# At each layer boundary, the sums of squares of x are taken as columns of tokens with the squares as weights, instead of as rows streamed through ones

## The chip, the cores and the metric

The kernel runs on one core of one Trainium2 chip. The metric is the device time of one launch in microseconds; the median of three runs is used. All arithmetic is fp32 (products are written as three fp32r products of high and low parts).

## The reference, cut to what matters

Two layers of a diffusion backbone over 512 latent tokens and 256 context tokens of width 1024 (layer 0 mixes with grouped-query attention, layer 1 with a Hyena long convolution; each is followed by a squared-ReLU MLP). Around every mixer and every MLP stands the same piece, and the change is in it:

```python
def rmsnorm(x, g):
    y = xf * lax.rsqrt(jnp.mean(xf * xf, axis=-1, keepdims=True) + RMS_EPS)
    return y * g
def sandwich_update(x, y_mix, mod, g, w1, w2):
    x = x + mod[2] * rmsnorm(y_mix, g[1])
    h = modulate(rmsnorm(x, g[2]), mod[3], mod[4])
    return x + mod[5] * rmsnorm(sq_relu_mlp(h, w1, w2), g[3])
```

So at the end of each mixer or MLP, y is normalised by its own root mean square and added to x, and x is normalised again for what comes next. The sum of squares of x over the 1024 channels, one number for each of the 512 tokens, is what the change computes in another way.

## The kernel before, in words

Activations are held transposed: x, y and the operands hhi and hlo are tiles of 128 channels by 8 chunks by 512 tokens. A weight matrix is cut into units: a unit is 8 chunks of 128 x 128 weights and gives 128 output channels for 512 tokens, with three products for each chunk (high by high, high by low, low by high; L1760, L1761, L1762 in the helper that the profile names). Each weight unit is loaded by SP, cut into high and low parts by ScalarE (L695) and VectorE (L1127), and multiplied by TensorE. The program of every engine is written out by hand, with semaphores between them; the order within an engine is the order of its code. There are four boundaries b = 0 to 3 (after attention, after MLP 0, after Hyena, after MLP 1). The last, b = 3, only adds y to x; the sums of squares of x are taken at the first three.

A boundary runs as follows (function `boundary` of each engine, and `first_units` of TensorE).

- **y's root.** TensorE's `square_column` (L1984) sums y's squares with a narrow product: the squares (128 x 128) are the weights, and one column of ones is streamed (L1989), after a product of 64 rows that writes zeros (L1987). An fp32 product is recorded as two matmuls, so a call with 4 columns of 128 tokens gives 8 records. ScalarE takes the root (L939), VectorE its reciprocal (L1451), and TensorE spreads it over 128 rows (`root_rows`, L1997). Around this, `keep_busy` (L2001, records at L2004) issues products of 512 columns whose result nobody reads: 3 before, 3 between, 10 after.
- **x.** VectorE scales y (`y_scale`, L1465) and adds it to x (`x_add`, L1470) in four parts: two halves of 256 tokens (`HALVES`), each in two groups of four chunks. ScalarE squares x into y's place (L951), two chunks at a time. TensorE sums the squares over the channels in `x_sums` (L2023, records at L2029): the weights are a 128 x 128 tile of ones, the squares of one chunk and half (128 x 256) are streamed, and 8 chunks accumulate in `XSUM[h]`, so that each of 128 rows holds all 256 sums.
- **x's root.** VectorE's `x_column` (L1472) turns the rows into columns of tokens: for each 128 tokens it multiplies the 128 x 128 block of the sums with the identity and adds along the row (L1477, then a read-out of the accumulator), which leaves the diagonal in `xcol`. ScalarE takes the root of two columns (`x_root`, L961), VectorE the reciprocal (`x_inverse`, L1484), TensorE spreads it to rows (`x_rows`, L2033, records at L2036).
- **Operands.** VectorE multiplies x by gain and root (`half_scaled`, L1488), ScalarE adds the shift and rounds to hhi (L969), VectorE gets hlo (`half_lo`, L1493).
- **First units.** TensorE then runs the first three units of the next matrix chunk by chunk for half 0 and then half 1 (`first_units`), with `x_rows` of half 1 after chunk 3 of half 0.

The order of VectorE within a boundary is: four parts of scale and add, with `x_column(0)` ahead of the last scale and `x_inverse(0)` ahead of the last add; then the products of half 0, with `x_column(1)` at chunk 3 and `x_inverse(1)` at chunk 5; then half 1. The order of TensorE is `x_sums(b, 0)`, the first four chunks of `x_sums(b, 1)`, `x_rows(b, 0)`, the last four chunks, the first units.

Of the kernel before, what the change touches and what calls it, by code (L numbers as in the profile page):

```python
# [27 lines left out]
ALU = mybir.AluOpType  # L28
ACT = mybir.ActivationFunctionType
AX = mybir.AxisListType  # L30

P = 128
D = 1024
KC = D // P
NT = 512
NC = 256
# [6 lines left out]
QT = NT // P  # L43
EPS = 1e-6
FH = 64
# [43 lines left out]
def build(nc, xT, ctxT, cT, cols, wpack, ahead, apack, fw1, fw2, fw3, featsT, skips, decay, tables, consts, ropes, fdram, out):  # L89
    with ExitStack() as ctx:  # L90
        def sb(name, shape, dt=F32, stack=ctx):
            return stack.enter_context(nc.sbuf_tensor(name, shape, dt))

        def sem(name):
            return ctx.enter_context(nc.semaphore(name))
# [17 lines left out]
        S = sb("scratch", [P, 12, NT])  # L113
# [12 lines left out]
        rq = sb("rq", [P, NH * QT])  # L126
        bmax = sb("bmax", [P, 2])
        nroot = sb("nroot", [P, QT])
        xcol = sb("xcol", [P, QT])
        xroot = sb("xroot", [P, QT])  # L130
        epst = sb("eps", [P, 1])
        tap2 = sb("tap2", [P, 2, NT])
        ident, ones = (cst[:, n, :] for n in range(2))
        y = S[:, 0:KC, :]
# [23 lines left out]
        with ExitStack() as area:  # L158
            t2hi = sb("t2hi", [P, 6, NT], F32R, area)
# [10 lines left out]
        B2 = ctx.enter_context(nc.psum_tensor("bank2", [P, NT], F32))  # L170
        B3 = ctx.enter_context(nc.psum_tensor("bank3", [P, NT], F32))
        SC = ctx.enter_context(nc.psum_tensor("bank45", [P, 2, NT], F32))
        SD = ctx.enter_context(nc.psum_tensor("bank67", [P, 2, NT], F32))
# [22 lines left out]
        inverse_done = sem("inverse_done")  # L196
        row_done = sem("row_done")
        xsum_done = sem("xsum_done")
        xcol_done = sem("xcol_done")
        xroot_done = sem("xroot_done")  # L200
        xinverse_done = sem("xinverse_done")
        xrow_done = sem("xrow_done")
# [120 lines left out]
        for u in range(QKV_UNITS):  # L323
            if u in UNIT_Q:
                h = UNIT_Q.index(u)
# [72 lines left out]
        FIRST_BANKS = (AB[:, 0, :], AB[:, 1, :], SC[:, 0, :], B2[:, :])  # L398
        X_GROUPS = 4
        HALVES = (slice(0, NC), slice(NC, NT))  # L400
        XSUM = (B2[:, 0:NC], SD[:, 0, 0:NC])
        XROWS = (SD[:, 1, 0:NC], SC[:, 1, 0:NC])

        def operand_base(b):
# [4 lines left out]
        def f(ap):  # L409
            return ap.bitcast(F32)  # L410
# [275 lines left out]
        def _(act):  # L686
            own = Own(act, own_act)
            A = nc.scalar.activation
# [147 lines left out]
            for t in range(QKV_UNITS + 2):  # L836
# [7 lines left out]
                for n, (_, ps, w, r, key, hi, lo) in jobs_of(t - 1):  # L844
# [3 lines left out]
                    else:  # L848
                        h, w = UNIT_Q.index(t - 1), QT
# [9 lines left out]
                for i, (n, (_, ps, w, r, key, hi, lo)) in enumerate(jobs_of(t)):  # L859
# [6 lines left out]
                    if key:  # L866
                        ins = A(value_of(n), ps, ACT.Copy)
                    else:
                        h = UNIT_Q.index(t)
                        if h >= 3:  # L870
                            act.wait_ge(job_full, jobs_of(UNIT_Q[h - 3])[0][1][3] + 1)
                        ins = A(value_of(n), ps, ACT.Copy, scale=qg[:, 0:1])
# [84 lines left out]

            def x_root(b, h):

                act.wait_ge(xcol_done, 4 * b + 2 * h + 2)  # L960
                A(xroot[:, 2 * h:2 * h + 2], xcol[:, 2 * h:2 * h + 2], ACT.Sqrt, scale=1.0 / D,  # L961
                  bias=epst[:, 0:1]).then_inc(xroot_done, 1)

            def half_his(b, h, js):
# [153 lines left out]
        def _(dve):  # L1118
# [299 lines left out]
            for n in range(NQ + 6):  # L1418
# [10 lines left out]
                if 0 <= m < NQ:  # L1429
                    dve.wait_ge(phi_done, m + 1)  # L1430
                    at = slice((m % 2) * P, (m % 2 + 1) * P)
# [16 lines left out]
            def inverse(m):  # L1448

                dve.wait_ge(root_done, m + 1)  # L1450
                nc.vector.reciprocal(nroot[:, :], nroot[:, :]).then_inc(inverse_done, 1)  # L1451

            def boundary(b):
                lo_, no_, ls, ts = BOUND[b][2:]
                inverse(b)
                if b % 2:
                    dve.wait_ge(yg_done, KC * (b // 2 + 1))
                else:
                    dve.wait_ge(evac_done, (U_OUT0, U_OUT1)[b // 2] + KC)
                dve.wait_ge(row_done, b + 1)  # L1460

                def y_scale(h, g):
                    at, js = HALVES[h], slice(4 * g, 4 * g + 4)
                    rows = B3[:, at].unsqueeze(1).broadcast_to([P, 4, NC])
                    TT(y[:, js, at], y[:, js, at], rows, ALU.mult).then_inc(scaled_done, 1)  # L1465

                def x_add(h, g):
                    at, js = HALVES[h], slice(4 * g, 4 * g + 4)
                    dve.wait_ge(scaled_done, X_GROUPS * b + 2 * h + g + 1)
                    TT(x[:, js, at], x[:, js, at], y[:, js, at], ALU.add).then_inc(x_done, 1)  # L1470

                def x_column(h):  # L1472
                    dve.wait_ge(xsum_done, 2 * b + h + 1)
                    for c in range(2):
                        if b or h or c:
                            dve.wait_ge(xcol_done, 4 * b + 2 * h + c)
                        nc.vector.tensor_tensor_reduce(S[:, 8, 0:P], XSUM[h][:, c * P:(c + 1) * P], ident, 1.0, 0.0,  # L1477
                                                       ALU.mult, ALU.add,
                                                       xcol[:, 2 * h + c:2 * h + c + 1]).then_inc(xcol_done, 1)

                def x_inverse(h):
                    dve.wait_ge(xroot_done, 2 * b + h + 1)
                    half = xroot[:, 2 * h:2 * h + 2]
                    nc.vector.reciprocal(half, half).then_inc(xinverse_done, 1)  # L1484

                def half_scaled(h, j):
                    at = HALVES[h]
                    STT(y[:, j, at], x[:, j, at], gcol(lo_, no_, j), XROWS[h], ALU.mult, ALU.mult).then_inc(ht_done, 1)  # L1488

                def half_lo(h, j):  # L1490
                    at = HALVES[h]
                    dve.wait_ge(hhi_done, operand_base(b) + KC * h + j + 1)
                    STT(hlo[:, j, at], y[:, j, at], shift(ls, ts, j), f(hhi[:, j, at]), ALU.add,  # L1493
                        ALU.subtract).then_inc(h_done, 1)

                if b == 3:
                    for i in range(X_GROUPS):
                        js = slice(2 * i, 2 * i + 2)
                        rows = B3[:, :].unsqueeze(1).broadcast_to([P, 2, NT])
                        TT(y[:, js, :], y[:, js, :], rows, ALU.mult).then_inc(scaled_done, 1)  # L1500
                        dve.wait_ge(scaled_done, X_GROUPS * b + i + 1)
                        TT(x[:, js, :], x[:, js, :], y[:, js, :], ALU.add).then_inc(x_done, 1)  # L1502
                    return
                y_scale(0, 0)
                x_add(0, 0)
                y_scale(0, 1)
                x_add(0, 1)
                y_scale(1, 0)
                x_add(1, 0)
                x_column(0)  # L1510
                y_scale(1, 1)
                x_inverse(0)
                x_add(1, 1)
                for h in range(2):
                    dve.wait_ge(xrow_done, 2 * b + h + 1)
                    dve.wait_ge(x_done, X_GROUPS * b + 2 * h + 2)
                    for j in range(KC + 1):
                        if j < KC:
                            half_scaled(h, j)
                        if j:  # L1520
                            half_lo(h, j - 1)
                        if h == 0 and j == 3:
                            x_column(1)
                        if h == 0 and j == 5:
                            x_inverse(1)
                    if h == 0:
                        prep(NEXT_UNIT[b] + AHEAD, AHEAD, AHEAD % 2)
# [40 lines left out]
            for j in range(OUT_UNITS):  # L1568
# [3 lines left out]
                if j in (1, 3, 5):  # L1572
                    third = j // 2
                    at = slice(2 * third, 2 * third + 2)
# [180 lines left out]
        def _(pe):  # L1755
            mm = nc.tensor.matmul
# [146 lines left out]
            for t in range(QKV_UNITS + 2):  # L1903
# [18 lines left out]
                for n, (_, ps, w, r, key, hi, lo) in jobs_of(t - 1):  # L1922
# [8 lines left out]
                    for qt in range(QT):  # L1931
                        ins = mm(B2[:, qt:qt + 1], S[:, 4 + n % 2, qt * P:(qt + 1) * P], ones[:, 0:1],  # L1932
                                 start=True, stop=True)
# [18 lines left out]
            for n in range(NQ + 5):  # L1952
                m = n - 3
                if 0 <= m < NQ:
                    pe.wait_ge(p_done, m + 1)
                    pe.wait_ge(exp_done, min(n - 1, NQ))
                    for kt in range(KT):
                        ins = nc.tensor.transpose(turned(m)[:, kt * P:(kt + 1) * P],  # L1958
                                                  PROB[m % 2][:, kt * P:(kt + 1) * P], ident)
                    ins.then_inc(pt_done, 1)  # L1960
                if n < NQ:
                    h, qt = divmod(n, QT)
# [43 lines left out]
            def boundary(b):  # L2006
                if b == 0:
                    pe.wait_ge(thi_done, 4)
                keep_busy(3)
                pe.wait_ge(yacc_done, (KC - 2) * (b + 1))  # L2010
                if b:
                    pe.wait_ge(xcol_done, 4 * b)
                if b == 2:
                    pe.wait_ge(tap_done, HY_UNITS)
                square_column(S[:, 11, :], True, False)
                pe.wait_ge(ysq_done, KC * (b + 1))
                square_column(S[:, 10, :], False, True).then_inc(col_done, 1)
                keep_busy(3)
                root_rows(b)
                if b < 3:  # L2020
                    keep_busy(10)

            def x_sums(b, h, js=range(KC)):  # L2023
                at = HALVES[h]
                if h == 0:
                    pe.wait_ge(root_done, b + 1)
                for j in js:
                    pe.wait_ge(xsquare_done, KC * b + 4 * h + j // 2 + 1)
                    ins = mm(XSUM[h], ones, y[:, j, at], start=j == 0, stop=j == KC - 1)  # L2029
                if js[-1] == KC - 1:  # L2030
                    ins.then_inc(xsum_done, 1)

# [244 lines left out]
```

## Time and profile before

| | before |
|---|---|
| median of 3 runs | 1406.29 us (1404.71 to 1406.71) |
| the profiled execution, its own time | 1407.46 us |
| its span, first to last instruction | 1405.7 us |
| TensorE busy | 1366.5 us, 97% |
| VectorE, ScalarE, GpSimd busy | 63%, 43%, 9% |
| granted clock of TensorE, mean | 0.993 of full speed |
| share of the chain that ended last | TensorE 84%, VectorE 7% |

The span is 1.8 us shorter than the execution's time. The busy time of an engine is the union of its instructions; a record of a matmul includes its way through the array, so that successive matmuls overlap, and what one costs is the step from its start to the next one's. The granted clock is a share of 2.4 GHz: 1.00 is 2.4 GHz and 0.50 is 1.2 GHz.

### The profile page before, as it was taken

What the parts mean: (1) busy time and instruction counts of PE and PEld (TensorE: products, weight loads), DVE (VectorE), ACT (ScalarE), POOL (GpSimd) and SP (SyncE); (2) the same over time, 40 slices, a digit from 0 to 9 for tenths busy, and PEclk for the clock granted to TensorE, in tenths of its full rate; (3) what the DMA queues carried; (4) which work ended last, traced back from release to release, by engine and by line L of the source; (5) the groups of instructions that cost most, each with busy time, mean ns of one, the idle gap of its engine ahead of it and who ended that gap; (6) DMA issues with size and microseconds to landing.
All of it is one profiled execution on the core that took longest, in us unless ns stands there. A gap on an engine that the chain in (4) does not pass through costs nothing.

```text
span 1405.7 us, 18116 instructions
## 1 busy us (share of the span) xinstructions
PE 1366.5 (97%) x6676; PEld 1124.2 (80%) x6676; DVE 890.2 (63%) x1279; ACT 608.4 (43%) x903; POOL 123.1 (9%) x151
## 2 busy tenths in 40 slices
PE   9989998999999999999999999999999999999996
PEld 2568787988888888888879888888888888888885
DVE  6898779977865555555457999997274333333333
ACT  3655446664462432514435433433446143341541
POOL 1761120002000000000110000000200000000011
PEclk9999999999999999999999999999999999999998
DMA  9535251119266565565321222231303222223221
GB/s 361 218 141 175 82 167 52 46 46 320 84 210 209 180 209 180 193 199 176 104 90 61 75 105 76 90 120 36 119 27 120 94 95 97 94 99 104 90 75 60
DMA packets 48330, 178.47 MB, mean 127 GB/s; under 512 B 5928, under 2 KB 6248, under 8 KB 45834
## 3 DMA queue, kind: packets, MB, share of 16 engines
q1 hardware_dynamic: 45194, 164.51, 34.3%
q0 software_dynamic: 3072, 13.11, 2.9%
q8 instruction: 39, 0.64, 0.2%
q14 instruction: 25, 0.20, 0.0%
HBM read 164.49 MB, written 10.49 MB: 124 GB/s over the span
## 4 chain that ended last, share of the span: by engine, by line
PE 84%; DVE 7%; issue 1%; ACT 1%; POOL 0%; DVEq 0%; POOLq 0%; ACTq 0%
PE bank L1760 27%; PE bank L1762 26%; PE bank L1761 26%; PE bank L1958 2%; PE bank L2029 1%; DVE x L1470 1%; DVE scratch L1465 1%; PE bank L1989 1%; PE bank L2004 0%; PE bank L1932 0%; PE bank L2111 0%; PE bank L1997 0%; DVE x L1502 0%; DVE glo L1663 0%; DVE scratch L1500 0%
## 5 line engine op out<-in xcount | busy, mean ns | idle before, releaser
L1760 PE MATMUL bank<-hhi,whi 128*128 128x512 f32 (+1 forms) x1000 | 376.8, 377 | 0.4 <-DVE wlo L1127 0.4
L1762 PE MATMUL bank<-hhi,wlo 128*128 128x512 f32 (+1 forms) x1000 | 374.2, 374 | 0.0
L1761 PE MATMUL bank<-hlo,whi 128*128 128x512 f32 (+1 forms) x1000 | 373.9, 374 | 0.0
L695 ACT ACTIVATE whi<-raw 128x1024 fp32r<-128x1024 f32 x180 | 189.1, 1053 | 231.8 <-PE bank L1762 199.9
L1127 DVE TENSOR_TENSOR wlo<-raw,whi 128x1024 fp32r<-128x1024 f32 x180 | 222.4, 1237 | 91.8 <-ACT whi L695 90.3
L1760 PEld LDWEIGHTS bank<-hhi,whi 128*128 128x128 f32 x1000 | 188.4, 188 | 34.0 <-issue 1.2
L1762 PEld LDWEIGHTS bank<-hhi,wlo 128*128 128x128 f32 x1000 | 188.3, 188 | 34.0
L1761 PEld LDWEIGHTS bank<-hlo,whi 128*128 128x128 f32 x1000 | 188.4, 188 | 32.8
L1762 PE MATMUL bank<-ghi,wlo 128*128 128x512 f32 x512 | 199.2, 389 | 0.0
L1760 PE MATMUL bank<-ghi,whi 128*128 128x512 f32 x512 | 199.2, 389 | 0.0
L1761 PE MATMUL bank<-glo,whi 128*128 128x512 f32 x512 | 199.2, 389 | 0.0
L1544 DVE TENSOR_TENSOR glo<-scratch,ghi 128x512 fp32r<-128x512 f32 x64 | 44.3, 693 | 173.7 <-ACT ghi L990 173.7
L1762 PEld LDWEIGHTS bank<-ghi,wlo 128*128 128x128 f32 x512 | 96.1, 188 | 20.1
L1761 PEld LDWEIGHTS bank<-glo,whi 128*128 128x128 f32 x512 | 96.1, 188 | 20.0
L1760 PEld LDWEIGHTS bank<-ghi,whi 128*128 128x128 f32 x512 | 96.1, 188 | 19.8
L662 POOL TENSOR_TENSOR scratch<-scratch 128x512 f32<-128x512 f32 x24 | 33.1, 1381 | 831.9 <-ACT scratch L917 831.9
L986 ACT ACTIVATE scratch<-bank 128x512 f32<-128x512 f32 x64 | 38.1, 596 | 151.8 <-PE bank L1762 151.8
L1556 DVE TENSOR_TENSOR scratch<-scratch,bank 128x512 f32<-128x512 f32 x48 | 33.0, 687 | 109.2 <-PE bank L1762 109.2
L1415 DVE CUSTOM_DVE_ANT_0 araw<-araw,crow 128x1024 f32<-128x1024 f32 x36 | 43.5, 1218 | 0.0
L1415 DVE CUSTOM_DVE_ANT_0 amore<-amore,crow 128x1024 f32<-128x1024 f32 x36 | 43.5, 1216 | 0.0
L988 ACT ACTIVATE scratch<-scratch 128x512 f32<-128x512 f32 x64 | 40.5, 632 | 2.0
L990 ACT ACTIVATE ghi<-scratch 128x512 fp32r<-128x512 f32 x64 | 40.5, 632 | 2.0
(275 smaller groups left out, 1968.7 us busy)
## 6 DMA issues: line engine op xcount, KB each, us to landing
raw<-in_wpack SPq DMA_DIRECT2D x180, 512.0 KB, 3.5
araw<-in_apack SPq DMA_DIRECT2D x40, 512.0 KB, 3.5
amore<-in_apack SPq DMA_DIRECT2D x36, 512.0 KB, 3.5
ablk<-in_ahead SPq DMA_DIRECT2D x8, 1024.0 KB, 11.6
spectra<-scratch SPq DMA_DIRECT2D x16, 512.0 KB, 3.2
araw<-spectra POOLq DMA_DIRECT2D x8, 1024.0 KB, 5.1
fs<-in_fw SPq DMA_DIRECT2D x2, 1024.0 KB, 11.2
x<-in_xT SPq DMA_DIRECT2D x1, 2048.0 KB, 12.5
```

Source lines behind the costliest of these rows:

```text
L662: nc.gpsimd.tensor_tensor(S[:, 11, :], S[:, 11, :], S[:, 10, :], ALU.add).then_inc(yacc_done, 1)
L695: A(whi[:, s, :], raw[:, r, :], ACT.Copy).then_inc(hi_done, 1)
L986: A(S[:, 8 + j % 2, :], bank, ACT.Relu).then_inc(evac_done, 1)
L988: A(S[:, 10 + j % 2, :], S[:, 8 + j % 2, :], ACT.Square).then_inc(g_full, 1)
L990: A(ghi[:, j, :], S[:, 10 + j % 2, :], ACT.Copy).then_inc(ghi_done, 1)
L1127: TT(wlo[:, s, :], raw[:, r, :], f(whi[:, s, :]), ALU.subtract).then_inc(lo_done, 1)
L1415: nc.vector.tensor_tensor_reduce(slot, slot, crow if early else crow1[:, :], 1.0, 0.0, ALU.mult, ALU.add, dst).then_inc(arow_done, 1)
L1544: TT(glo[:, j, :], S[:, 10 + j % 2, :], f(ghi[:, j, :]), ALU.subtract).then_inc(g_done, 1)
L1556: TT(y[:, j, :], y[:, j, :], AB[:, j % 2, :], ALU.add).then_inc(evac_done, 1)
L1760: mm(o, lh, rh, start=first, stop=False)
L1761: mm(o, lh, rl, start=False, stop=False)
L1762: return mm(o, ll, rh, start=False, stop=last)
```

## The change

The row sums of x become column sums. In `x_sums`, the squares of one chunk and 128 tokens are the weights and one column of ones is streamed, into one column for each 128 tokens (`XCOLS[h]`, two columns of a bank). Ahead of each half a product of 64 rows writes zeros into the two columns. After every second chunk one product of 256 columns is issued whose result nobody reads. ScalarE's `x_root` reads the two columns where they are and waits for the sums; `x_column`, the tile `xcol` and the semaphore `xcol_done` are gone. At the start of a later boundary TensorE waits for the roots of the one before it instead of its columns.

```diff
-        XSUM = (B2[:, 0:NC], SD[:, 0, 0:NC])
+        XCOLS = (B2[:, 0:2], SD[:, 0, 0:2])
...
             def x_root(b, h):
 
-                act.wait_ge(xcol_done, 4 * b + 2 * h + 2)
-                A(xroot[:, 2 * h:2 * h + 2], xcol[:, 2 * h:2 * h + 2], ACT.Sqrt, scale=1.0 / D,
+                act.wait_ge(xsum_done, 2 * b + h + 1)
+                A(xroot[:, 2 * h:2 * h + 2], XCOLS[h], ACT.Sqrt, scale=1.0 / D,
                   bias=epst[:, 0:1]).then_inc(xroot_done, 1)
...
-                def x_column(h):
-                    dve.wait_ge(xsum_done, 2 * b + h + 1)
-                    for c in range(2):
-                        if b or h or c:
-                            dve.wait_ge(xcol_done, 4 * b + 2 * h + c)
-                        nc.vector.tensor_tensor_reduce(S[:, 8, 0:P], XSUM[h][:, c * P:(c + 1) * P], ident, 1.0, 0.0,
-                                                       ALU.mult, ALU.add,
-                                                       xcol[:, 2 * h + c:2 * h + c + 1]).then_inc(xcol_done, 1)
-
...
                 x_add(1, 0)
-                x_column(0)
                 y_scale(1, 1)
...
-                        if h == 0 and j == 3:
-                            x_column(1)
...
                 if b:
-                    pe.wait_ge(xcol_done, 4 * b)
+                    pe.wait_ge(xroot_done, 2 * b)
...
                 if h == 0:
                     pe.wait_ge(root_done, b + 1)
+                if js[0] == 0:
+                    mm(XCOLS[h], ones[0:FH, :], ident[0:FH, P - 2:P], start=True, stop=False)
                 for j in js:
                     pe.wait_ge(xsquare_done, KC * b + 4 * h + j // 2 + 1)
-                    ins = mm(XSUM[h], ones, y[:, j, at], start=j == 0, stop=j == KC - 1)
+                    for c in range(2):
+                        ins = mm(XCOLS[h][:, c:c + 1], y[:, j, at][:, c * P:(c + 1) * P], ones[:, 0:1], start=False,
+                                 stop=j == KC - 1 and c == 1)
+                    if j % 2:
+                        mm(SC[:, 0, 0:NC], t2hi[:, 0, 0:P], t2hi[:, 1, 0:NC], start=True, stop=True)
                 if js[-1] == KC - 1:
                     ins.then_inc(xsum_done, 1)
```

## Rows read from the trace of the kernel before

**Rows 1.** The page: busy time of each engine, and the chain by line.

```profile
PE 1366.5 (97%) x6676; PEld 1124.2 (80%) x6676; DVE 890.2 (63%) x1279; ACT 608.4 (43%) x903; POOL 123.1 (9%) x151
...
PE bank L1760 27%; PE bank L1762 26%; PE bank L1761 26%; PE bank L1958 2%; PE bank L2029 1%; DVE x L1470 1%; DVE scratch L1465 1%; PE bank L1989 1%; PE bank L2004 0%; PE bank L1932 0%; PE bank L2111 0%; PE bank L1997 0%; DVE x L1502 0%; DVE glo L1663 0%; DVE scratch L1500 0%
```

**Rows 2.** Busy time by stretch (start:end, length, engines), the first boundary and its first units.

```profile
361.00:371.46 10.46, 8.01 (x35) 6.35 (x36) 9.17 (x15) 5.58 (x11) 0.00 (x0) 1.00 0.00 1
371.49:389.30 17.81, 17.81 (x150) 17.78 (x149) 13.22 (x35) 8.71 (x17) 0.00 (x0) 1.00 0.10 31
```

**Rows 3.** The line of x's sums, all of its matmuls (ns min/median/max, starts).

```profile
L2029 PE MATMUL bank<-scratch,consts x96: 379/379/483, 361.8 to 1037.0; 128*128 128x256 f32 x96
```

**Rows 4.** Timeline of the first boundary (start us, us, engine, line; idle before, releaser).

```profile
358.14 2.56 PE L2004 MATMUL bank<-t2hi 128*128 128x512 f32 x10
...
364.08 1.99 PE L2029 MATMUL bank<-scratch,consts 128*128 128x256 f32 x8 [0.33 <-ACT scratch L951]
364.52 1.23 DVE L1470 TENSOR_TENSOR x<-x,scratch 128x1024 f32<-128x1024 f32 x1
...
366.11 0.29 DVE L1477 CUSTOM_DVE_ANT_0 scratch<-bank,consts 128x128 f32<-128x128 f32 x1 [0.36 <-PE bank L2029]
...
366.47 1.99 PE L2029 MATMUL bank<-scratch,consts 128*128 128x256 f32 x8 [0.40 <-ACT scratch L951]
...
366.84 0.28 ACT L961 ACTIVATE xroot<-xcol,eps 128x2 f32<-128x2 f32 x1
367.79 0.16 DVE L1484 RECIPROCAL xroot<-xroot 128x2 f32<-128x2 f32 x1
...
368.08 0.63 PEld L2036 LDWEIGHTS bank<-consts,xroot 128*128 128x128 f32 x4
...
369.05 0.87 DVE L1488 SCALAR_TENSOR_TENSOR scratch<-x,gain,bank 128x256 f32<-128x256 f32 x2
369.17 1.15 ACT L951 ACTIVATE scratch<-x 128x512 f32<-128x512 f32 x2 [2.04 <-DVE x L1470]
...
369.85 1.99 PE L2029 MATMUL bank<-scratch,consts 128*128 128x256 f32 x8 [0.94 <-ACT scratch L951]
...
370.75 0.48 DVE L1493 SCALAR_TENSOR_TENSOR hlo<-scratch,mods,hhi 128x256 fp32r<-128x256 f32 x1 [0.83 <-ACT hhi L969]
...
371.49 0.47 PE L1760 MATMUL bank<-hhi,whi 128*128 128x256 f32 x1
```

**Rows 5.** Timeline of y's column sums, at the first and the second boundary.

```profile
354.64 1.95 PE L1989 MATMUL bank<-consts,scratch 128*128 128x1 f32 x16
...
356.63 0.26 ACT L939 ACTIVATE nroot<-bank,eps 128x4 f32<-128x4 f32 x1 [1.72 <-PE bank L1989]
356.99 0.18 DVE L1451 RECIPROCAL nroot<-nroot 128x4 f32<-128x4 f32 x1 [2.40 <-ACT nroot L939]
...
722.05 0.38 PE L1987 MATMUL bank<-consts 64*128 64x4 f32 x2
...
724.17 1.39 PE L2004 MATMUL bank<-t2hi 128*128 128x512 f32 x3
```

**Rows 6.** Busy time by stretch; behind POOL's, the granted clock of TensorE.

```profile
352.39:359.22 6.83, 6.83 (x43) 5.70 (x42) 3.04 (x8) 1.44 (x3) 0.00 (x0) 1.00 0.81 301
721.03:724.45 3.42, 3.42 (x24) 2.94 (x23) 1.43 (x6) 1.46 (x3) 0.00 (x0) 1.00 0.95 370
724.45:727.86 3.41, 3.41 (x13) 3.03 (x12) 0.66 (x2) 0.16 (x1) 0.00 (x0) 0.50 0.16 64
...
1390.05:1393.45 3.40, 2.70 (x11) 2.21 (x9) 0.77 (x2) 0.10 (x1) 0.00 (x0) 0.50 0.00 0
```

**Rows 7.** Timeline, the eight broadcasts of y's root at the first and second boundary.

```profile
357.23 1.15 PE L1997 MATMUL bank<-consts,nroot 128*128 128x128 f32 x8
...
725.35 1.91 PE L1997 MATMUL bank<-consts,nroot 128*128 128x128 f32 x8
```

More of the change, by code:

```diff
@@ L128, in build @@
         nroot = sb("nroot", [P, QT])
-        xcol = sb("xcol", [P, QT])
         xroot = sb("xroot", [P, QT])
@@ L198, in build @@
         xsum_done = sem("xsum_done")
-        xcol_done = sem("xcol_done")
         xroot_done = sem("xroot_done")
```

## The prediction

> **What bounds the kernel.** I read the page first: TensorE is busy 97% of the span, and 79% of the chain that ended last is the three products of a unit, L1760 to L1762 [rows 1]. So a microsecond counts only if TensorE loses it. The page's line of the granted clock is not flat, so I read the clock by stretches later. Then I read the table of stretches around one boundary. In the 10.46 us from the first scaled x to the end of its sums TensorE has 8.01 us busy; in the 17.81 us of the first units behind it, it is busy throughout; the clock is full in both [rows 2]. VectorE and ScalarE are ahead once the first units run, so what the change saves them there is worth nothing. What matters is when the first unit starts, and at what clock TensorE gets there. The line of the sums has 96 records, 32 at each of three boundaries [rows 3], so each term below comes three times. The timeline of the first one follows; the others repeat it to 0.02 us.
>
> **The path in that boundary** [rows 4]. TensorE sums half 0 (eight records, 364.08 to 366.07). VectorE takes the diagonal twice, 366.11 on, then does the last scaling, the reciprocal (367.79) and the last add of x. ScalarE squares (369.17), TensorE sums the last four chunks (369.85), and the first unit's first matmul starts at 371.49. Its operand is ready sooner: hlo starts at 370.75 and takes 0.48, so 371.23. In this last step TensorE itself is the bound.
>
> **Removed and added, at full clock.** (1) Sums. A wide block of four chunks is 8 records; from its first to the next weights is 1.61 us (366.47 to 368.08, where the rows of roots load theirs) [rows 4]. A narrow record, a square as weights and one column streamed, is that of L1989: 16 in 1.95 us, the last 0.25, so (1.95 - 0.25)/15 = 0.113 us each [rows 5]. A new block is 16 of them and 2 fillers of 256 columns. No such filler is in the trace; bounds are 0.12, what a 256-column product of the first units takes (150 records in 17.81 us [rows 2]), and 0.26, what each of the ten 512-column fillers takes (2.56 us together) [rows 4]. I take 0.12, of the same width. 16 x 0.113 + 2 x 0.12 = 2.05 us, or 0.44 more than before, per block. The zeroing product of two columns costs about what L1987 does, 0.38 us [rows 5], and for both halves is issued while TensorE waits for squares: nothing. If that cover went, it would be 0.3 us.
> (2) Half 0's sums: 364.08 + 2.05 = 366.13 for the last narrow one's end, against 366.07. A narrow result reaches ScalarE 0.04 us after its end (L1989 ends 356.59, the root starts 356.63 [rows 5]), but ScalarE's own squares hold the root at 366.84 as before [rows 4]. Reading PSUM instead of a column costs it nothing: 0.26 us at L939 [rows 5] against 0.28.
> (3) Two diagonals leave VectorE, about 0.3 us each, and with them the 0.36 us of waiting before them [rows 4]. The scaling starts behind the add of 364.52, that is at 365.7. It ends before the root, for which the reciprocal now waits: 366.84 + 0.28 + 0.10 for the signal (what lies between 356.63 + 0.26 and the reciprocal at 356.99 [rows 5]) = 367.22, instead of 367.79. Late next is that root. The last add and its squares come 0.57 us earlier, the last block starts at 369.28 instead of 369.85 and ends at 369.28 + 2.05 = 371.33 against 371.47: a gain of 0.14.
> (4) The rows of roots wait behind the longer block on TensorE: 366.47 + 2.05 = 368.52 instead of 368.08. They reach VectorE at 369.3, not 369.05. Queued behind that wait are half 0's products and ScalarE's hhi; hhi stands behind ScalarE's squares anyway (368.60 + 1.15 = 369.75), so hlo is done at 370.8, still 0.5 us ahead of TensorE.
> (5) Half 1's diagonals (0.6 us of VectorE at 372.7) lie under the first units: nothing. No DMA changes, the SP and POOL queues are not touched, and the new wait before the next boundary's columns (roots done, not columns done) was met hundreds of microseconds before.
> Sum at full clock: 3 x -0.14 = -0.4 us; from 0 to -1.7 (if all of the 0.57 came through).
>
> **The clock.** Not one wide matmul is left between the ten fillers that end at 360.7 [rows 4] and the first unit, but eight of 256 columns and four broadcasts. The trace shows what narrow ones do. From 721.03 to 724.45 TensorE is busy 3.42 of 3.42 us, most of it (722.05 to 724.17 [rows 5]) narrow records between wide fillers, at the full 2.4 GHz; the next stretch, 724.45 to 727.86, is granted 0.50, that is 1.2 GHz. At the last boundary the same work is followed by 0.50 from 1390.05. At the first it leaves the clock at 1.00 [rows 6]. So 2 us of narrow records among wide ones cost the clock in some of the blocks. The new stretch is 10 us long, at all three boundaries. I forecast that it falls in each.
> The Trainium skill ("TensorE: Matmul & The Clock Gate", Why this matters for your kernels) ties a fall to idle gaps between bursts of matmuls; TensorE would have no gap much over 1 us in the new boundary, so by that rule the clock holds and the time is that of the second rival, 1405.9. The trace does not agree: TensorE was never without work from 721.03 to 724.45 and its clock fell [rows 6].
> Price: eight broadcasts take 1.15 us at 2.4 GHz, 1.91 at 1.2 [rows 7]: with the last one's 0.28 and 0.42 taken off, (1.91 - 0.42)/7 = 0.213 us a record instead of (1.15 - 0.28)/7 = 0.12, for the same loads of 128 weights that bound a narrow record, which goes from 0.113 to the same 0.213. So a block costs 18 x 0.10 = 1.8 us more, the rows of roots 0.4. The falls shown come 2.4 us after narrow work began (722.05 to 724.45); here it begins at 361.7, so a fall may come from 363 to 367, and I take 366. Block 1.8, rows 0.4, block 1.8, less 0.35 because no wait for squares is left between, less 0.14: the first unit starts 3.5 us later, at 375.0. One low stretch lasts 3.41 us [rows 6], so the third would begin at 372.8 and end at 376.2: 1.2 us of first units at half speed, 0.6 lost: 4.1 us. If that third one, mostly narrow, is followed by a fourth, 1.7 more: 5.8. I take the middle, 4.9. Ends: two low stretches only, 2 x 1.7 less 0.35 and what else was idle, 2.6; four, with the fall before 364 so that the root is late too, 7.2. Behind the boundary TensorE bounds, so nothing is won back.
> Sum: 3 x 4.9 = 14.7. The profiled execution took 1407.46 (span 1405.7 and 1.8 around it), 1.2 above the median; it would be 1422.2, and for the median 1406.3 + 14.7 = 1421.0. Ends 3 x 2.6 and 3 x 7.2: 1414 and 1428.
>
> **Rivals.** A measurement tells about 0.2%, 2.8 us, from no change.
> - **Falls only in part**: at one or two boundaries, or a single low stretch each (1.7 less the 0.5 that is idle now, three times 1.2). The block at 354 that kept its clock speaks for it; that the new stretch is four times as long against. 1409 to 1414, chance 0.20.
> - **The clock holds**: fillers or weight loads are enough. For it: two fillers in every block, and no moment without weights. Against: three 512-column fillers ahead of the narrow records of 722 and more behind them were not enough. 1406.3 - 0.4 = 1405.9, chance 0.14.
> - **Faster**: the clock holds, and the operands that VectorE makes, not TensorE's sums, set the pace from the start of the first unit on. Then all that VectorE is rid of counts: four diagonals of 0.3 us and the wait of 0.36, 1.6 us at each boundary, 4.8 in all: 1401.5. It decides from the point where the last block takes less than 1.5 us, since hlo is there at 370.8: (1.5 - 0.24)/16 = 0.08 for a narrow record, against the 0.113 of L1989. Chance 0.04.
>
> **The numbers.** Forecast (falls at all three, two to four low stretches each) 0.62, in part 0.20, holds 0.14, faster 0.04. Range 1409 to 1429: it takes in the first two and leaves out 0.18. Slower by over 0.2% is 0.62 + 0.20 = 0.82; within 0.2% 0.14; faster 0.04.
>
> **What would show it.** In the profile after: no rows of the diagonal; narrow records of the sums at 0.11 us, later at 0.21; the granted clock 0.50 for some 7 to 10 us from about 366, and likewise near 735 and 1032; the first unit starts at 375 instead of 371.5. In the half where the clock is full, the last add comes 0.5 us earlier. The forecast is wrong if the clock stays at 1.00 between the sums and the first unit; then the first unit should start at 371.3.

## The result, and the profile after

| | before | after |
|---|---|---|
| median | 1406.50 us (4 runs, 1404.71 to 1407.98) | 1424.62 us (4 runs, 1423.08 to 1428.05) |
| profiled execution, its own time | 1407.46 us | 1425.49 us |
| its span | 1405.7 us | 1423.4 us |
| granted clock, mean | 0.993 | 0.977 |

The changed kernel is slower: ratio 1.0136, 95% interval 1.0123 to 1.0149; by the medians 18.1 us. 1421.0 was forecast, 1409 to 1429 was the range.

The page after: busy time of each engine, the granted clock in 40 slices, and the chain by line (L1746 to L1748 are the three products that were L1760 to L1762; L2018 is the narrow record of x's sums, L2021 its filler).

```profile
PE 1390.2 (98%) x6808; PEld 1152.0 (81%) x6808; DVE 887.7 (62%) x1255; ACT 608.5 (43%) x903; POOL 123.2 (9%) x151
...
PEclk9999999999799999999998999999979999999998
...
PE bank L1746 26%; PE bank L1748 26%; PE bank L1747 26%; PE bank L2018 2%; PE bank L1944 2%; PE bank L2021 1%; PE bank L1975 1%; PE bank L1918 0%; DVE x L1468 0%; PE bank L1990 0%; DVE scratch L1463 0%; PE bank L2103 0%; DVE x L1491 0%; DVE glo L1649 0%; DVE scratch L1489 0%
```

VectorE has 2.5 us less to do than in [rows 1], and that changed nothing. TensorE is busy 23.7 us longer although it streams far fewer columns. The first three dents in the line of the clock lie in the slices of the three boundaries; the 8 in the last slice stands in the page of the kernel before too. The busy time by stretch, changed kernel, shows them in full (the number behind POOL's is the granted clock):

```profile
358.02:362.54 4.52, 3.84 (x24) 3.05 (x22) 4.10 (x4) 1.15 (x2) 0.00 (x0) 1.00 0.04 15
362.54:383.02 20.48, 20.48 (x96) 20.24 (x96) 13.33 (x24) 8.76 (x17) 0.00 (x0) 0.50 0.00 1
383.02:397.84 14.82, 14.82 (x126) 14.82 (x126) 6.56 (x16) 4.50 (x9) 0.00 (x0) 1.00 0.10 36
...
741.42:755.07 13.65, 13.65 (x64) 13.41 (x63) 8.84 (x20) 6.24 (x14) 0.00 (x0) 0.50 0.01 1
...
1034.97:1038.38 3.41, 3.41 (x14) 3.07 (x13) 1.17 (x1) 0.00 (x0) 0.00 (x0) 0.50 0.00 0
...
1045.21:1058.86 13.65, 13.65 (x65) 13.63 (x65) 9.22 (x21) 6.79 (x14) 0.00 (x0) 0.50 0.00 1
```

At each boundary TensorE runs at 1.2 GHz for 13.65 or 20.48 us, where [rows 2] has 1.00 throughout. It is without a pause in these stretches. The other three executions of the changed kernel have a mean granted clock of 0.975 to 0.978, like this one. The timeline of the first boundary, changed kernel, to be laid beside [rows 4]; its last two lines are where the narrow records of the second and third boundary begin:

```profile
361.56 1.05 PE L2018 MATMUL bank<-consts,scratch 128*128 128x1 f32 x8 [0.68 <-ACT scratch L949]
...
362.79 1.70 PE L2018 MATMUL bank<-consts,scratch 128*128 128x1 f32 x8
...
368.37 0.26 ACT L959 ACTIVATE xroot<-bank,eps 128x2 f32<-128x2 f32 x1 [1.55 <-PE bank L2018]
368.66 0.17 DVE L1473 RECIPROCAL xroot<-xroot 128x2 f32<-128x2 f32 x1 [1.90 <-ACT xroot L959]
...
373.20 1.06 PE L2028 MATMUL bank<-consts,xroot 128*128 128x128 f32 x4
...
374.30 0.87 DVE L1477 SCALAR_TENSOR_TENSOR scratch<-x,gain,bank 128x256 f32<-128x256 f32 x2 [4.35 <-PE bank L2028]
...
375.35 0.48 DVE L1482 SCALAR_TENSOR_TENSOR hlo<-scratch,mods,hhi 128x256 fp32r<-128x256 f32 x1 [0.18 <-ACT hhi L967]
...
377.89 0.41 PE L1746 MATMUL bank<-hhi,whi 128*128 128x256 f32 x1
378.11 0.41 PE L1747 MATMUL bank<-hlo,whi 128*128 128x256 f32 x1
378.32 0.41 PE L1748 MATMUL bank<-hhi,wlo 128*128 128x256 f32 x1
...
737.84 1.05 PE L2018 MATMUL bank<-consts,scratch 128*128 128x1 f32 x8 [0.71 <-ACT scratch L949]
...
1040.40 1.05 PE L2018 MATMUL bank<-consts,scratch 128*128 128x1 f32 x8
```

Eight narrow records take 1.05 us ahead of the fall and 1.70 behind it. The fall comes 0.98 us after the first narrow record at this boundary, 3.58 and 4.81 us after it at the other two. The root of half 0 comes at 368.37 instead of 366.84, now because its sums are late. VectorE waits 4.35 us for the rows of roots, and the first unit starts at 377.89 instead of 371.49. It does not wait for its operand (375.35 + 0.48), but for TensorE's own sums.

To compare executions I measure each boundary from the first of the ten fillers to the first unit, and on to the first product of 512 columns, with which the three first units are over. Each is the difference of two starts in the timeline:

| | to the first unit | to the end of the first units | low clock up to that end |
|---|---|---|---|
| before | 13.35, 13.46, 13.35 | 31.25, 31.35, 31.24 | 0, 0.94, 0 |
| after | 19.88, 18.25, 17.33 | 39.82, 37.07, 37.13 | 20.48, 13.65, 13.65 + 1.62 |

The three boundaries lost 8.57, 5.72 and 5.89 us, 20.2 in all. The span grew by 17.7, because elsewhere this execution was 2.5 us shorter. 1.5 of them lie at y's sums, ahead of the fillers of the three boundaries and in the last boundary: the kernel before had stretches at 0.50 at 724.45 and 1390.05 [rows 6], and this execution of the changed kernel had none where they stood, only one at 1034.97. Another 0.8 lie between the second and the third boundary, in the products from 820 to 968 of the kernel before, and 0.1 ahead of the first boundary; the change has no code in either place, and their cause is open.

### The profile page after: what moved, and what is told of

Its sections match the earlier page's. It is cut to its first block, busy times and chain, and to the rows that moved or that the text cites. A ratio compares the mean times of both kernels' runs of the same rounds, so it can differ in the third digit from the quotient of the medians.

```text
span 1423.4 us, 18348 instructions
## 1 busy us (share of the span) xinstructions
PE 1390.2 (98%) x6808; PEld 1152.0 (81%) x6808; DVE 887.7 (62%) x1255; ACT 608.5 (43%) x903; POOL 123.2 (9%) x151
## 4 chain that ended last, share of the span: by engine, by line
PE 85%; DVE 6%; issue 1%; ACT 1%; POOL 0%; DVEq 0%; POOLq 0%; ACTq 0%
PE bank L1746 26%; PE bank L1748 26%; PE bank L1747 26%; PE bank L2018 2%; PE bank L1944 2%; PE bank L2021 1%; PE bank L1975 1%; PE bank L1918 0%; DVE x L1468 0%; PE bank L1990 0%; DVE scratch L1463 0%; PE bank L2103 0%; DVE x L1491 0%; DVE glo L1649 0%; DVE scratch L1489 0%
## 5 line engine op out<-in xcount | busy, mean ns | idle before, releaser
L1746 PE MATMUL bank<-hhi,whi 128*128 128x512 f32 (+1 forms) x1000 | 378.9, 379 | 0.5 <-DVE wlo L1125 0.4
L1748 PE MATMUL bank<-hhi,wlo 128*128 128x512 f32 (+1 forms) x1000 | 376.5, 377 | 0.0
L1746 PEld LDWEIGHTS bank<-hhi,whi 128*128 128x128 f32 x1000 | 191.3, 191 | 34.0 <-issue 1.3
L1748 PEld LDWEIGHTS bank<-hhi,wlo 128*128 128x128 f32 x1000 | 190.9, 191 | 33.9
L1746 PE MATMUL bank<-ghi,whi 128*128 128x512 f32 x512 | 199.2, 389 | 0.0
L1748 PE MATMUL bank<-ghi,wlo 128*128 128x512 f32 x512 | 199.2, 389 | 0.0
L1748 PEld LDWEIGHTS bank<-ghi,wlo 128*128 128x128 f32 x512 | 96.1, 188 | 20.0
L1746 PEld LDWEIGHTS bank<-ghi,whi 128*128 128x128 f32 x512 | 96.1, 188 | 19.9
```

The source lines that it names most:

```text
L1746: mm(o, lh, rh, start=first, stop=False)
L1748: return mm(o, ll, rh, start=False, stop=last)
```

## The experiments

Theory A: the loss is TensorE at 1.2 GHz, because next to nothing is streamed. Theory B: it is the records and weight loads themselves and the roots that come late behind them. Each kernel was compared with the kernel before on the same chip (1406.3 us in both groups of runs). All stretches and times from traces are those of the one profiled execution of a kernel.

**More columns, same records.** `e1_cols128` has 128 columns of ones streamed past each block of squares; the root reads every 128th column, and the zeroing product (not in this cut) is 256 columns wide instead of 2. It computes the same.

```diff
-        XCOLS = (B2[:, 0:2], SD[:, 0, 0:2])
+        XWIDE = (B2[:, 0:256], SD[:, 0, 0:256])
+        XCOLS = tuple(a[:, 0:256:128] for a in XWIDE)
...
-                        ins = mm(XCOLS[h][:, c:c + 1], y[:, j, at][:, c * P:(c + 1) * P], ones[:, 0:1], start=False,
+                        ins = mm(XWIDE[h][:, c * 128:(c + 1) * 128], y[:, j, at][:, c * P:(c + 1) * P], ones[:, 0:128],
```

> As the changed kernel, but each square block, as weights, has 128 columns of ones streamed past it instead of one: same records, same weight loads, same fillers, only more streamed columns. A record should still step by 0.11 us, since the broadcasts of 128 columns do. Theory A (the loss is TensorE at 1.2 GHz, because next to nothing is streamed): the granted clock stays at 1.00 between the ten fillers and the first unit at all three boundaries, a block of four chunks takes about 2.05 us, the first unit starts near 371.4, and the time is about 1406 (1404.5 to 1408.5). Theory B (the loss is the number of records and weight loads, and roots that come late behind them): nothing of that is changed, so 1420 or more.

Measured: 1404.42 us, ratio 0.9990 (0.9981 to 1.0000), 0.1 us below the range that I gave for theory A, and not told apart from the kernel before beyond doubt. The first and the third boundary by stretch, up to the first unit, and the line of the sums, `e1_cols128`:

```profile
356.51:369.88 13.37, 12.88 (x93) 11.14 (x92) 11.21 (x13) 5.66 (x11) 0.00 (x0) 1.00 0.06 21
369.88:387.60 17.72, 17.72 (x150) 17.72 (x149) 12.70 (x31) 8.65 (x17) 0.00 (x0) 1.00 0.09 31
...
1022.41:1035.90 13.49, 13.10 (x92) 11.35 (x92) 11.21 (x13) 5.66 (x11) 0.00 (x0) 0.98 0.00 0
```

```profile
L2019 PE MATMUL bank<-consts,scratch x192: 271/275/377, 360.1 to 1035.7; 128*128 128x128 f32 x192
```

192 records as in the changed kernel, and the clock stays up; the 0.98 is the end of a stretch that began behind y's sums. The first unit starts 13.37 us after the start of the fillers, where the changed kernel has 19.88. With the narrow records and their weight loads unchanged in number, 20.2 us are back. Theory B is out: the wider zeroing product is more work, not less.

**Without the fillers.** `e2_cols128_nofill` is the same without the two lines `if j % 2:` and the product of 256 columns under it.

> As e1_cols128 and without the product of 256 columns after every second chunk. Theory A: clock still 1.00, a block 16 x 0.113 = 1.8 us, the first unit 0.2 to 0.4 us earlier than in e1_cols128 at each boundary; about 1405 (1404 to 1407), level with the kernel before or up to 0.1% faster. Theory B: 24 records fewer at 0.12 to 0.21 us each, 1416 to 1421.

Measured: 1403.17 us, ratio 0.9983 (0.9972 to 0.9993): faster than the kernel before, by 0.8 us more than the range for theory A allowed. The first unit starts after 12.89, 12.79 and 12.89 us, about 0.5 us sooner than before. The fillers of the first and third boundary ran in part at 0.50, in stretches that began behind y's sums; the second boundary, undisturbed, reads

```profile
727.38:740.16 12.78, 12.07 (x85) 10.20 (x84) 11.09 (x13) 5.66 (x11) 0.00 (x0) 1.00 0.00 0
```

**More filler.** `e3_wide_fillers` keeps the narrow records and lets TensorE do more that nobody reads.

```diff
                     if j % 2:
-                        mm(SC[:, 0, 0:NC], t2hi[:, 0, 0:P], t2hi[:, 1, 0:NC], start=True, stop=True)
+                        for i in range(3):
+                            mm(SC[:, 0, :], t2hi[:, 0, 0:P], t2hi[:, 1 + i, :], start=True, stop=True)
```

> As the changed kernel, narrow records kept, but after every second chunk three fillers of 512 columns instead of one of 256: more work for TensorE that nobody reads. Theory A: the clock holds at 1.00; a block takes 16 x 0.113 + 6 x 0.23 = 3.2 us instead of the 1.61 of the kernel before, the last block starts later too because the rows of roots wait behind the second one, so 1.5 to 3.5 us a boundary: 1411 to 1417, faster than the changed kernel although it does more. Theory B: slower than the changed kernel by the added work, 1430 or more.

Measured: 1430.47 us (1425.66 to 1435.66), ratio 1.0189 (1.0156 to 1.0223). My number was missed, and the number alone would speak for theory B. The stretches, `e3_wide_fillers`, tell why:

```profile
356.59:373.94 17.35, 16.65 (x110) 14.50 (x108) 12.37 (x16) 6.51 (x13) 0.00 (x0) 1.00 0.03 9
732.99:760.30 27.31, 27.31 (x106) 24.61 (x105) 13.05 (x24) 8.65 (x17) 0.00 (x0) 0.50 0.00 1
1039.27:1056.60 17.33, 16.66 (x109) 14.50 (x108) 12.37 (x16) 6.50 (x13) 0.00 (x0) 1.00 0.01 1
```

At the first and the third boundary the clock held. There the narrow records cost only TensorE time: the first unit starts after 17.35 us, 4.0 more than before. I had said 1.5 to 3.5, having reckoned the longer block twice and not four times; with 3.2 us each all four follow one another almost without a pause. At the second boundary the clock fell all the same and stayed low for 27.31 us, and that boundary alone lost 16.3 us. The profiled execution is the fastest of the four; in the two slowest (1434.17 and 1435.66 us) the mean granted clock was 0.979 and 0.980 against 0.986 here, so the clock was low for longer in them, at places that no trace shows. So fillers between narrow records hold the clock sometimes, at a price that is over half of the 6.7 us that a fall cost on average in the changed kernel.

**Without the diagonals.** `e4_no_diagonal` is the kernel before with `x_column` left out and the root taken of the first two columns of the streamed sums. This leaves out which token a sum belongs to; it sizes what was to be had.

```diff
-                A(xroot[:, 2 * h:2 * h + 2], xcol[:, 2 * h:2 * h + 2], ACT.Sqrt, scale=1.0 / D,
+                A(xroot[:, 2 * h:2 * h + 2], XSUM[h][:, 0:2], ACT.Sqrt, scale=1.0 / D,
...
-                x_column(0)
...
-                            x_column(1)
```

> The kernel before without the diagonals on VectorE: ScalarE takes the root of the first two columns of the streamed sums, which leaves out the choice of each token's own sum. It shows what the diagonals cost when nothing else changes. Theory A: the last add comes 0.57 us earlier, the last block starts and ends 0.57 us earlier, clock at 1.00: 3 x 0.57 = 1.7 us less, about 1404.7, at most 3 us less. Theory B, by which roots that come late are what costs: the same or a little more, 1403 to 1405; the run does not tell the two apart but sizes the gain that was to be had.

Measured: 1403.51 us, ratio 0.9983 (0.9974 to 0.9993). In the timeline of `e4_no_diagonal` the fillers start at 357.58; the reciprocal and the first unit are

```profile
366.67 0.17 DVE L1484 RECIPROCAL xroot<-xroot 128x2 f32<-128x2 f32 x1 [0.24 <-ACT xroot L961]
...
370.31 0.47 PE L1757 MATMUL bank<-hhi,whi 128*128 128x256 f32 x1
```

The reciprocal comes 9.09 us after the fillers' start instead of 9.65 [rows 4], 0.56 sooner, and the first unit after 12.73 instead of 13.35. But 2.31 us of these fillers ran at 0.50, behind y's sums. At the third boundary, at full clock in both kernels, the reciprocal comes after 8.98 instead of 9.65 us, 0.67 sooner where 0.57 was forecast, and the first unit after 12.62 instead of 13.35. That is all the diagonals are worth: 0.6 to 0.8 us a boundary (0.62, 0.83, 0.73).

**Half of the stretch.** `e5_half1_narrow` takes half 0 as before, with its diagonals, and half 1 as the changed kernel does.

```diff
+                    if h == 0:
+                        ins = mm(XSUM0, ones, y[:, j, at], start=j == 0, stop=j == KC - 1)
+                        continue
                     for c in range(2):
```

> Half 0 as in the kernel before (streamed rows, diagonals on VectorE), half 1 as in the changed kernel (columns, zeroing product, fillers). The narrow stretch is then about 5 us, from 366.5 to 371.5, instead of 10. Theory A: the clock falls at some boundaries or stays low for less; 1408 to 1418, and the stretches at 0.50 in the trace account for it. Theory B (a cost for each narrow record): half of the changed kernel's loss, 1415.

**A quarter of the columns.** `e6_cols32` is `e1_cols128` with 32 in place of 128.

> As e1_cols128 with 32 columns of ones streamed past each block of squares instead of 128; records and weight loads as in the changed kernel. Theory A: between e1_cols128 (1404.4) and the changed kernel (1424.6); if a quarter of the columns is still too little, the clock falls in the same places as in the changed kernel and the time is 1415 or more; if it is enough, 1405. Theory B is out since e1_cols128; a weaker form of it (the fill time of each record, not the clock) expects what e1_cols128 gave, 1404.4.

Measured: `e5_half1_narrow` 1417.14 us, ratio 1.0081 (1.0066 to 1.0097); `e6_cols32` 1421.20 us, ratio 1.0105 (1.0090 to 1.0121). Their low stretches, first `e5_half1_narrow`, then `e6_cols32`:

```profile
367.32:377.56 10.24, 9.83 (x47) 9.54 (x46) 8.26 (x19) 5.99 (x12) 0.00 (x0) 0.50 0.01 2
739.37:749.61 10.24, 9.95 (x47) 9.66 (x46) 8.39 (x19) 5.98 (x12) 0.00 (x0) 0.50 0.01 2
1039.74:1049.98 10.24, 9.62 (x46) 9.44 (x45) 8.03 (x19) 5.98 (x12) 0.00 (x0) 0.50 0.00 0
```

```profile
368.15:378.39 10.24, 10.24 (x50) 10.24 (x50) 7.12 (x18) 5.86 (x12) 0.00 (x0) 0.50 0.00 0
740.20:750.44 10.24, 10.24 (x50) 10.24 (x50) 6.96 (x18) 4.79 (x11) 0.00 (x0) 0.50 0.01 2
1040.58:1054.23 13.65, 13.65 (x64) 13.31 (x64) 8.87 (x20) 7.23 (x15) 0.00 (x0) 0.50 0.00 1
```

With the narrow half alone the clock fell at every boundary, and 32 columns did not hold it either. The weaker form of theory B, for which 32 columns were as good as 128, is out too. The 1417.14 us of `e5_half1_narrow` by themselves would also be near the 1415 of theory B, which is out since `e1_cols128`; it is the trace that tells. The low time accounts for the loss of all of them. Fillers to the end of the first units, three boundaries together, against the 93.84 us of the kernel before. The low clock counted is that of the falls that began behind the fillers; the ends of stretches that began behind y's sums lie under the ten fillers, where 2.03 us of them in `e2_cols128_nofill` left the first unit 0.10 us later than in its undisturbed boundary, and are left out:

| | low clock of these falls | lost there | lost per us of low clock |
|---|---|---|---|
| changed kernel | 47.8 | 20.2 | 0.42 |
| e6_cols32 | 34.1 | 14.9 | 0.44 |
| e5_half1_narrow | 30.7 | 13.3 | 0.43 |
| e1_cols128 | 0 | -0.4 | |

**y's sums too.** Where the first three boundaries of `e2_cols128_nofill` still fell, it was behind y's sums, which stream one column as well. `e8_xy_cols128` streams 128 there too, `e9_y_cols128` does only that, in the kernel before.

```diff
-                A(nroot[:, :], B2[:, 0:QT], ACT.Sqrt, scale=1.0 / D, bias=epst[:, 0:1]).then_inc(root_done, 1)
+                A(nroot[:, :], B2[:, 0:NT:P], ACT.Sqrt, scale=1.0 / D, bias=epst[:, 0:1]).then_inc(root_done, 1)
...
-                    ins = mm(B2[:, c:c + 1], src[:, c * P:(c + 1) * P], ones[:, 0:1], start=False,
+                    ins = mm(B2[:, c * P:(c + 1) * P], src[:, c * P:(c + 1) * P], ones, start=False,
...
-                keep_busy(3)
+                keep_busy(1)
...
+                mm(B2[:, :], ones[0:FH, :], ident[0:FH, P - 1:P].to_broadcast([FH, NT]), start=True, stop=False)
```

> As e2_cols128_nofill, and y's column sums too stream 128 columns instead of one (the zeroing product of 512 columns stands ahead of the wait in place of two of the three 512-column fillers). Theory A: the falls that come behind y's sums in some boundaries (724.45 and 1390.05 in the kernel before) go; about one fall of 1.2 to 1.7 us less in a run; 1401.5 to 1403.5 against e2_cols128_nofill's 1403.2, about 0.25% faster than the kernel before. If those falls have another cause they stay, and the time is 1403 to 1404.

> The kernel before, x's sums streamed as they were, with only y's column sums streaming 128 columns, as in e8_xy_cols128. Theory A: no stretch at 0.50 behind y's sums at the boundaries; 1404.5 to 1406, against 1406.3. Otherwise 1406.3.

Measured: `e8_xy_cols128` 1402.47 us, ratio 0.9973 (0.9964 to 0.9983); `e9_y_cols128` 1405.40 us, ratio 0.9996 (0.9987 to 1.0005). The three boundaries of `e8_xy_cols128`, from the last weights ahead of y's sums to the end of the first units:

```profile
352.00:389.02 37.02, 36.31 (x268) 32.67 (x267) 26.57 (x50) 15.74 (x31) 0.00 (x0) 1.00 0.21 78
719.50:756.45 36.95, 36.25 (x267) 32.60 (x266) 26.00 (x51) 15.92 (x31) 0.00 (x0) 1.00 0.16 58
1014.00:1050.93 36.93, 36.24 (x268) 32.65 (x267) 24.09 (x44) 15.74 (x31) 0.00 (x0) 1.00 0.09 30
```

The first unit starts 12.79 us after the start of the fillers at all three, and none of the three has a low stretch; the last boundary is low from 1389.98 on, as the others' ends are. In `e9_y_cols128` the three boundaries are at 1.00 as well, but its interval holds 1. Its trace says why nothing is gained: from the last product of weights ahead of y's sums to the first of the ten fillers it takes 5.21, 5.21 and 5.14 us, the kernel before 4.83, 5.89 and 4.76. The fall at 724.45 cost about 1.1 us there (1.2 and 1.3 in `e1_cols128`, which has 4.82, 6.04 and 6.12), but the zeroing product of 512 columns costs 0.38 at every boundary. `e8_xy_cols128` is faster than the kernel before beyond doubt, and it is not told apart from `e2_cols128_nofill`.

## Why the prediction was right, and where it was off

- **Full-clock terms** (1) to (4). The narrow record at 0.11 us and the block of 2.05 us held: in the changed kernel eight take 1.05 us at full clock, and eight of 128 columns in `e1_cols128` 1.05 to 1.16; its last block takes 2.02 (367.86 to 369.88). The first unit there starts 13.37 us after the start of the fillers against 13.35, where I had a gain of 0.14. What failed is the zeroing product "issued while TensorE waits for squares: nothing": ahead of half 1 it stands in the way. In `e1_cols128` it is 256 columns wide and holds TensorE from 364.66 to 365.29, though the first squares are there at 364.78; in the changed kernel, 2 columns wide, it takes 0.37 us (1045.02 to 1045.39) with the squares there at 1045.14. So most of the cover whose loss I priced at 0.3 was gone for that half. Term (3) was 0.10 short: `e4_no_diagonal` gains 0.67 for its 0.57. That the longer sums take this away again, as forecast, `e1_cols128` shows. Term (5), nothing under the first units, is borne out by `e4_no_diagonal`: at the third boundary 0.73 us is gained up to the first unit and 0.72 up to the end of the first units.
- **The fall**: at all three boundaries, as forecast. That it comes of streaming next to nothing is shown by `e1_cols128`, in which the narrow records differ in nothing but the streamed columns. The rule of the Trainium skill ("TensorE: Matmul & The Clock Gate", Why this matters for your kernels), by which idle gaps bring the fall, would have had the clock hold; the trace does not agree, with 20.48 us of 20.48 busy at 0.50.
- **The step that was mis-sized** is the price of a fall: "I take the middle, 4.9". Measured were 8.57, 5.72 and 5.89, a mean of 6.7, so 20.2 instead of 14.7 in this execution and 18.1 by the medians. At the second and third boundary the clock was low for 13.65 us, which is my case of four stretches of 3.41, priced at 5.8: that price held, and only the choice of the middle between three and four was wrong. The first boundary was low for 20.48 us, beyond anything I had priced. Its fall came at 362.54, not 366, so half 0's sums and its root were late as well, which I had kept for the end of the range (7.2); and the first units had already run for 5 us at half speed (377.89 to 383.02) when the clock came back. My 366 stood on one delay of 2.4 us behind the start of narrow work; here the delays were 0.98, 3.58 and 4.81. That the total still came within 4 us is in part luck: this execution was 2.5 us shorter outside the three boundaries.
- **The rivals.** "Falls only in part" and "the clock holds" are both refuted by the changed kernel's own trace. The price of "faster", 1.6 us a boundary, was not tested: it asked for a last block under 1.5 us, and the shortest here, 1.8 us in `e2_cols128_nofill` (738.36 to 740.16), still ends 0.15 us after the operand is ready. The 0.5 us a boundary that this kernel gains come by way of term (3): VectorE's last add, and with it the last block, comes sooner.

## What to carry to other kernels

A rearrangement that saves another engine's work by making TensorE's matmuls narrow has to be priced at the clock that the narrow ones leave behind, not at the record's length: look in the trace of the kernel before for a stretch where such matmuls ran between wide ones, and at the granted clock of the next stretch. If weights take as long to load as 128 columns to stream, stream the 128 columns, even if 127 results are copies: here it cost nothing (0.11 us a record either way) and was worth 20 us. Fillers between narrow matmuls are the weaker remedy; three of 512 columns for each eight records cost 4.0 us a boundary at full clock, and at one of three boundaries of the profiled execution they did not hold it.

## What the runs showed of the hardware that was not expected

- TensorE's clock can stay at half for 27.31 us while the engine has a record in every moment (`e3_wide_fillers`, 732.99 to 760.30), though 22 fillers of 512 columns began in it; the same program held 1.00 at its other two boundaries.
- A low stretch costs 0.42 to 0.44 us for each of its microseconds, not half. The records do not take twice as long: one of the first units steps by 0.213 us at half clock (377.89 to 378.32 for two) and by 0.12 at full clock, 1.8 times, which by itself makes 0.44. That waits for squares are filled as well is likely (TensorE idles 2.45 of the 10.46 us in [rows 2], 0.49 of 13.37 in `e1_cols128` and not at all in the changed kernel's low stretches), but it was not told apart.
- What exactly makes the clock fall or come back stays open. The fall came 0.98 to 4.81 us after the first narrow record. With the change's own fillers, one column and 32 columns a record lost the clock at every boundary, and 128 never did behind the ten fillers; nothing between 32 and 128 was tried.
